# Choosing an expert's rows with channels on the partitions at once, in a two-layer decoder step

## The reference

```
logits = x @ router;  top_v, top_i = top_k(logits, 2);  gate = softmax(top_v) at top_i
for e in range(8):
    y = y + gate[:, e] * ((silu(x @ wg[e]) * (x @ wu[e])) @ wd[e])
x = layer_norm(alpha * x + y)
```

## Time and profile before

| what | value |
|---|---|
| median of 3 runs | 1303.0 us (1302.25 to 1303.61) |
| the profiled execution's own time | 1302.67 us |
| its span, first to last instruction | 1300.9 us |
| TensorE matmul busy | 1243.0 us, 96% |
| TensorE weight load busy | 1158.3 us, 89% |
| VectorE busy | 1027.0 us, 79% |
| ScalarE busy | 825.3 us, 63% |
| mean granted TensorE clock | 0.992 |
| HBM read | 330.44 MB, 256 GB/s over the span |

### The profile page before, as it was taken

One profiled execution on the slowest core, in us unless ns is written; L12 is line 12 of the kernel. 1 busy time (PEld: TensorE's weight loads), 2 busy tenths in 40 slices (PEclk: granted clock), 3 DMA queues, 4 the chain that ended last, 5 costly groups with the idle time before them and its releaser, 6 DMA issues.

```text
span 1300.9 us, 22335 instructions
## 1 busy us (share of the span) xinstructions
PE 1243.0 (96%) x8651; PEld 1158.3 (89%) x8651; DVE 1027.0 (79%) x1064; ACT 825.3 (63%) x979; POOL 5.4 (0%) x22
## 2 busy tenths in 40 slices
PE   6999999999998899999999999999999999999992
PEld 4899999989988689989989989989998999998991
DVE  6687444467996688888888888889889879888886
ACT  3636563344876657767767767767776776776771
POOL 0000000000000000000000000000000000000000
PEclk9999999999999999999999999999999999999997
DMA  9355544422565169989989989999999998998931
GB/s 252 98 167 177 154 153 155 147 85 65 174 216 182 65 212 366 362 280 366 365 276 361 364 292 352 364 316 322 365 322 318 367 353 284 367 362 278 367 117 38
DMA packets 249537, 332.65 MB, mean 256 GB/s; under 512 B 6404, under 2 KB 222820, under 8 KB 249450
## 3 DMA queue, kind: packets, MB, share of 16 engines
q1 hardware_dynamic: 249283, 331.28, 75.8%
q10 hardware_dynamic: 199, 0.62, 0.2%
HBM read 330.44 MB, written 2.84 MB: 256 GB/s over the span
## 4 chain that ended last, share of the span: by engine, by line
PE 84%; DVE 10%; ACT 3%; issue 2%; DMA 0%; DVEq 0%; SPq 0%; ACTq 0%
PE bank L1088 36%; PE bank L1108 19%; PE bank L915 17%; PE bank L946 6%; DVE cacc L1368 2%; PE bank L1052 2%; PE bank L1097 1%; PE bank L1073 1%; ACT w_hi L546 1%; PE bank L854 1%; DVE acc L1533 1%; PE bank L900 1%; DVE sg L1265 1%; DVE yy_lo L1583 1%; DVE w_lo L1185 1%
## 5 line engine op out<-in xcount | busy, mean ns | idle before, releaser
L1185 DVE TENSOR_TENSOR w_lo<-raw,w_hi 128x2048 fp32r<-128x2048 f32 x309 | 707.8, 2291 | 184.3 <-ACT w_hi L546 183.6
L546 ACT CAST w_hi<-raw 128x2048 fp32r<-128x2048 f32 x309 | 591.1, 1914 | 226.1 <-PE bank L915 76.5
L1088 PE MATMUL bank<-w_hi,xg_hi 128*128 128x256 f32 x1408 | 400.7, 285 | 5.5 <-DVE acc L1533 3.7
L1088 PE MATMUL bank<-w_hi,xg_lo 128*128 128x256 f32 x1408 | 393.3, 279 | 0.0
L1088 PE MATMUL bank<-w_lo,xg_hi 128*128 128x256 f32 x1408 | 393.1, 279 | 0.0
L1088 PEld LDWEIGHTS bank<-w_hi,xg_hi 128*128 128x128 f32 x1408 | 264.5, 188 | 13.3 <-issue 9.1
L1088 PEld LDWEIGHTS bank<-w_lo,xg_hi 128*128 128x128 f32 x1408 | 265.0, 188 | 3.2
L1088 PEld LDWEIGHTS bank<-w_hi,xg_lo 128*128 128x128 f32 x1408 | 264.2, 188 | 0.0
L915 PE MATMUL bank<-x_hi,w_hi 128*128 128x304 f32 (+1 forms) x544 | 166.0, 305 | 6.9 <-DVE x_lo L1272 3.6
L915 PE MATMUL bank<-x_hi,w_lo 128*128 128x304 f32 (+1 forms) x544 | 164.0, 302 | 0.0
L915 PE MATMUL bank<-x_lo,w_hi 128*128 128x304 f32 (+1 forms) x544 | 163.2, 300 | 0.0
(11 more groups left out here) (202 smaller groups left out, 1279.5 us busy)
## 6 DMA issues: line engine op xcount, KB each, us to landing
raw<-in_moe_w_gate_dram SPq DMA_DIRECT2D x88, 1024.0 KB, 5.6
raw<-in_moe_w_up_dram SPq DMA_DIRECT2D x88, 1024.0 KB, 6.0
raw<-in_moe_w_down_dram SPq DMA_DIRECT2D x88, 1024.0 KB, 5.2
raw<-in_conv_w_dram SPq DMA_DIRECT2D x12, 1024.0 KB, 5.6
raw<-in_ffn_w_gate_dram SPq DMA_DIRECT2D x11, 1024.0 KB, 5.3
raw<-in_ffn_w_up_dram SPq DMA_DIRECT2D x11, 1024.0 KB, 5.4
raw<-in_ffn_w_down_dram SPq DMA_DIRECT2D x11, 1024.0 KB, 4.9
poolw<-in_pool_w_dram SPq DMA_DIRECT2D x1, 1024.0 KB, 10.8
```

Of the source, the lines that this page charges most:

```text
L546: act.copy(w_hi[t % SPLIT][:], raw[raw_slot(t)][:]).then_inc(hi_ready, 1)
L1088: last = pe.matmul(bank[:, 0:TW], x[:, c, :], w[:, c, :], start=(c == 0 and k == 0), stop=(c == KC - 1 and k == 2))
L1185: dve.tensor_tensor(w_lo[t % SPLIT][:], raw[raw_slot(t)][:], w_hi[t % SPLIT][:], ALU.subtract).then_inc(split_ready, 1)
```

## The change

The two steps `gather_rows` and `gather_turn` become one `gather`, at the place of `gather_rows`. The operands trade places: a block of 128 channels of `xn_hi` or `xn_lo` is stationary, and `sel` with its 128 places is moving. The result has the channels on the partitions at once. For each of the 8 channel blocks there are 6 matmuls (3 blocks of rows, high and low). The third block contracts over its 32 rows only. ScalarE's `rows_evac` and the buffer `xg_rows` go. The semaphore `gathered` is raised after each half, as before.

```
-            def gather_rows(g):
+            def gather(g):
                 pe.wait_ge(sel_ready, g + 1)
-                for i in range(3):
-                    if i == 2:
-                        pe.wait_ge(xlo_done, 3 * KC + 6)
-                    for m, x in enumerate((xn_hi, xn_lo)):
-                        for half in range(2):
-                            last = pe.matmul(ps[1 + 2 * half][:, :], sel[:, i, :],
-                                             x[:, i, half * HALF:(half + 1) * HALF],
-                                             start=(i == 0 and m == 0), stop=(i == 2 and m == 1))
-                last.then_inc(rows_gathered, 1)
-            def gather_turn(g):
                 for half in range(2):
-                    pe.wait_ge(rows_out, 2 * g + 2)
                     for c in range(4):
                         f = (4 * half + c) * P
-                        last = pe.transpose(ps[1 + 2 * half][:, c * P:(c + 1) * P], xg_rows[:, f:f + P], ident[:])
+                        for i in range(3):
+                            if half == 0 and c == 0 and i == 2:
+                                pe.wait_ge(xlo_done, 3 * KC + 6)
+                            m = OUT_ROWS[i]
+                            for x in (xn_hi, xn_lo):
+                                last = pe.matmul(ps[1 + 2 * half][:, c * P:(c + 1) * P], x[0:m, i, f:f + P],
+                                                 sel[0:m, i, :], start=(i == 0 and x is xn_hi),
+                                                 stop=(i == 2 and x is xn_lo))
                     last.then_inc(gathered, 1)
...
                         if j == NJ - 1 and not last:
-                            gather_rows(n + 1)
+                            gather(n + 1)
                         down(j - 1, g + 2)
                 turn_h(NJ - 1)
-                if not last:
-                    gather_turn(n + 1)
                 down(NJ - 1, T_MOE + TE - 1)
...
-                if not last:
-                    rows_evac(n + 1)
                 turn_evac(NJ - 1)
```

More of the change, by code:

```diff
@@ L220, in build_trunk @@
         yy_lo = area("yy_lo", [P, D], F32R, 4096)
-        xg_rows = area("xg_rows", [P, D], F32, 0)
         sel = area("sel", [P, 3, P], F32R, 8192)
@@ L294, in build_trunk @@
         sel_ready = sem("sel_ready")
-        rows_gathered = sem("rows_gathered")
-        rows_out = sem("rows_out")
         gathered = sem("gathered")
@@ L750, in xg_evac @@
                              ps[1 + 2 * k][:, :].rearrange("p (c n) -> p c n", c=4)).then_inc(xg_hi_done, 1)
[L752 to L756, removed]
             def one_expert(r, e, last):
@@ L797, in one_pass @@
             def one_pass(r):
-                rows_evac(r * E)
                 xg_evac(r * E)
@@ L1146, in one_expert @@
                         if j == NJ - 1 and not last:
-                            gather_rows(n + 1)
+                            gather(n + 1)
                         down(j - 1, g + 2)
                 turn_h(NJ - 1)
-                if not last:
-                    gather_turn(n + 1)
                 down(NJ - 1, T_MOE + TE - 1)
             def one_pass(r):
-                gather_rows(r * E)
-                gather_turn(r * E)
+                gather(r * E)
                 with pe.Fori(0, E - 1) as e:
```

## The result

The changed kernel takes 1377.5 us (median of 4 runs, 1376.9 to 1378.2) against 1303.3 us, a ratio of 1.0557 [1.0536, 1.0578]. The profiled execution took 1377.35 us (span 1375.6), 74.7 us more than that of before. The forecast was 1322.4 us, its range 1309 to 1342: the direction was right, the size was not, by nearly four times (74.2 us in place of 19.7).

The account below looks back on a forecast made before the run. TensorE's stream was taken to bound the expert stage. Looped gathers +18.4, gaps +0.6 and first gather +0.66 made +19.7 us on 1302.67, so 1322.4 us; own range 1319 to 1325, 8-in-10 range 1309 to 1342.

Parts of the forecast that it names:

- What bounds: In the expert stage, a microsecond added to TensorE's stream is a microsecond of the kernel, unless it falls into a gap.
- Turns and copies are worth nothing: Removing the eight turns before the last down block and a looped gather's two ScalarE copies (1.08 us) saves nothing.
- The extra 0.09 us: Before each last down block, removing the turns enlarges TensorE's gap by 0.09 us, +0.6 us over 7 experts.
- Loads set 0.112 us: In looped gathers, weight loads space the 48 short matmuls 0.112 us apart: +2.63 us each, +18.4 us for 7.
- Rivals 1 to 3: Gather loads hidden, 1301.6 to 1303.5 us (7 in 100); partly hidden, 1305 to 1319 (8); doubled instructions, 1364.8 (10).
- The 16 whose contraction is 32 rows ... I give them no discount.: In each gather, the 16 matmuls contracting over 32 rows were costed at the same 0.112 us as the others.
- rival 4: In gathers, load and columns in series, 1341.6 us, or clock halved in next down block, 2.75 us each; 5 in 100.
- First gather +0.66 us: At the gather ahead of the expert loop, the first expert matmul comes at 456.74 in place of 456.08, +0.66 us.
- the gaps: TensorE's idle time before the last down block of 7 experts, forecast to grow by 0.6 us in all.

Follow-up runs that it names:

- e1: The changed kernel with the third row block contracted over all 128 rows, as in every other contraction of the gather; 1329.6 us, ratio 1.0183.
- e4: The kernel before with 6 of the 8 turns of the gathered rows left out; 1305.6 us, ratio 1.0008.
- e5: e1 with every gather matmul contracted over 32 rows; 1353.1 us in one run.
- e6: e1 with 64 moving columns in place of 128 in the gather; 1350.1 us in one run.
- e9: e1 with 9 unused matmuls ahead of the first gather and 7 behind it, in TensorE's waits; 1324.3 us, ratio 1.0142.

## Why the prediction was wrong

- **What bounds.** Right. TensorE's stream sets the expert's time; nothing took the added time back. The expert period grew by 2.6 us in e1 (105.5), as forecast, and by 9.2 us in the changed kernel (112.1 against 102.9).
- **Turns and copies are worth nothing.** Right for the turns (e4). The copies had no run of their own, but in e1, which has neither, the period grew by just what the gather and the down block behind it did (2.56 + 0.04 us). The extra 0.09 us was not there, 0.6 us in all.
- **Loads set 0.112 us.** Right: 0.111 in e1, e5, e6. Rivals 1 to 3 fall with it. The 81 ns that the Trainium skill gives (page TensorE: Matmul & The Clock Gate, section Back-to-back issue gap) are not reached here either; the measured 0.111 us decides. With 128 rows and the clock held (e9) the kernel takes 19.2 us more than before on the same chip, against my 19.7.
- **"The 16 whose contraction is 32 rows ... I give them no discount."** The first failed step. I asked whether they were cheaper and never whether they were dearer: 16 changes of height at 0.145 us are 2.3 us for each gather, 16.2 us in all. The trace of before hardly has such a change in a dense stream, so this was an operation without a row, and I gave it no upper bound. The Trainium skill, page TensorE: Matmul & The Clock Gate, section LDWEIGHTS, says that a 32-row load takes as long as a 128-row one. The spacing of 0.111 us in e5 agrees; what cost time was the change between the two heights.
- **The clock.** The second failed step, and the larger: 14.5 us in the gathers, 15.2 in the down blocks, and most of the 9.8 at the first gather. I had it as half of rival 4 with 5 in 100, and priced it at 2.75 us a gather, the down block alone; it also doubled the rest of the gather. My argument was that the clock stood at 1.00 through the first gather with matmuls busy 4.09 of 7.00 us. But 12 of these 20 matmuls had 512 columns, and all of them 128 rows. The Trainium skill, the same page, section What's actually happening, puts the clock down to "how busy the PE has been recently". The record's busy time does not show that: it is 2.50 of 2.50 us in the stretch behind the fall, at a clock of 0.50. The clock fell with few rows (e5) and with few columns (e6) at the same spacing of starts.
- **First gather +0.66 us.** Wrong by the clock too. The pause behind the fourth matmul was there (449.73 to 450.46), and behind it the clock was 0.50. With the clock held (e9) it costs 0.9 to 1.5 us. So it is partly luck that e9's 19.2 us lie so near to my 19.7: the gathers are 0.5 us and the gaps 0.6 us cheaper than I had them, the first gather dearer.

The cause is settled by steps, each against before on its own chip: equal heights (e1) bring the added time from 74.2 to 24.1 us, and the held clock at the first gather (e9) brings it to 19.2. What stays open is how much of the 30 us of looped clock loss comes from the idle rows and how much from the pauses.

## What to carry to other kernels

Short matmuls cost their weight load, 0.111 us here, whatever they stream, and a long neighbour hides only one of them. Before cutting a matmul to fewer moving columns or fewer contracted rows, ask what the stream leaves idle in the array: the busy column won't show it, the clock column will, and part of the bill is paid by whatever comes next. In a dense stream, contract over zero rows rather than change the height: here that one line was worth 50 of 74 us.

## What was not expected of the hardware

- A change of contraction height between 128 and 32 or 64 rows delays the following starts by 0.15 us in a stream of 128-column matmuls; with 512 columns one costs 0.22 us.
- The clock fell in or just behind gathers with 64 rows or with 64 columns while matmul records covered all the time, and in six of seven with 88 columns.
